# Softmax's division by the row sums: from a VectorE multiplication to a diagonal matrix in the transposing products

## The reference, cut to what matters

```python
def attend(q, k, v):
    s = jnp.einsum("bqkgd,bskd->bkgqs", q, k, preferred_element_type=F32) * (B_HEAD_DIM ** -0.5)
    p = jax.nn.softmax(s, axis=-1).astype(v.dtype)
    return jnp.einsum("bkgqs,bskd->bqkgd", p, v)
```

## Time and profile before

| | us |
|---|---|
| median of 3 runs | 2290.29 |
| lowest and highest of them | 2287.31, 2292.7 |
| the profiled execution, its own time | 2290.72 |
| its span, first to last instruction | 2288.9 |
| granted TensorE clock in it | 0.996 |

### The profile page before, as it was taken

The page is one execution under the profiler, slowest core; times in us unless marked ns, Lnnn a source line. Parts: engine busy times, 40 slices in busy tenths (PEclk is TensorE's granted clock), DMA queues, the critical chain, the costliest instruction groups (busy, mean ns, idle before and its releaser), DMA issues.

```text
span 2288.9 us, 41418 instructions
## 1 busy us (share of the span) xinstructions
PE 2220.6 (97%) x17332; PEld 2045.3 (89%) x17332; DVE 1618.4 (71%) x2749; ACT 1156.7 (51%) x1937; POOL 153.3 (7%) x142
## 2 busy tenths in 40 slices
PE   7999999999989999999999999999999999999998
PEld 3665889998879999999999989997779999999998
DVE  4399668655977645798557687577988557799654
ACT  3425445443365446756346564345556345957343
POOL 0013000000000000000000000015630000000000
PEclk9999999999999999999999999999999999999999
DMA  8148054555244554415554325562025554514552
GB/s 346 73 183 317 37 221 166 185 186 201 92 166 168 187 186 171 173 57 184 184 182 157 141 93 203 184 221 74 19 94 183 184 184 169 183 55 166 185 184 92
DMA packets 50873, 368.46 MB, mean 161 GB/s; under 512 B 5632, under 2 KB 5888, under 8 KB 6528
## 3 DMA queue, kind: packets, MB, share of 16 engines
q1 hardware_dynamic: 50544, 363.72, 43.2%
q10 hardware_dynamic: 144, 2.10, 0.2%
HBM read 364.75 MB, written 1.05 MB: 160 GB/s over the span
## 4 chain that ended last, share of the span: by engine, by line
PE 81%; DVE 11%; ACT 5%; issue 2%; DMA 0%; SPq 0%; DVEq 0%; POOL 0%; ACTq 0%
PE psum L263 67%; DVE weight_rest L257 2%; PE psum L4508 1%; PE psum L3069 1%; PE psum L4509 1%; ACT weight_parts L221 1%; PE psum L4530 1%; PE psum L3703 1%; PE psum L2719 1%; DVE work L2021 1%; PE psum L4544 1%; DVE work L3533 1%; DVE spare L2509 0%; DVE work L2508 0%; DMA weight_ring<-stream_dram 0%
## 5 line engine op out<-in xcount | busy, mean ns | idle before, releaser
L263 PE MATMUL psum<-input_parts,weight_parts 128*128 128x256 f32 x5184 | 933.0, 283 | 6.0 <-DVE work L1489 1.8
L263 PEld LDWEIGHTS psum<-input_parts,weight_parts 128*128 128x128 f32 x5184 | 801.0, 189 | 11.2 <-issue 5.3
L263 PE MATMUL psum<-input_parts,weight_rest 128*128 128x256 f32 x2592 | 733.6, 283 | 0.0
L257 DVE TENSOR_TENSOR weight_rest<-weight_ring,weight_parts 128x1024 fp32r<-128x1024 f32 x528 | 621.1, 1222 | 151.8 <-ACT weight_parts L221 151.3
L221 ACT ACTIVATE weight_parts<-weight_ring 128x1024 fp32r<-128x1024 f32 x540 | 538.1, 1051 | 128.2 <-PE psum L263 105.6
L263 PEld LDWEIGHTS psum<-input_parts,weight_rest 128*128 128x128 f32 x2592 | 488.9, 189 | 0.0
L263 PE MATMUL psum<-hidden_parts,weight_parts 128*128 128x256 f32 x2496 | 450.7, 283 | 2.6 <-DVE weight_rest L257 1.3
L263 PEld LDWEIGHTS psum<-hidden_parts,weight_parts 128*128 128x128 f32 x2496 | 385.1, 189 | 6.0 <-issue 3.4
L263 PE MATMUL psum<-hidden_parts,weight_rest 128*128 128x256 f32 x1248 | 352.2, 282 | 0.0
L263 PEld LDWEIGHTS psum<-hidden_parts,weight_rest 128*128 128x128 f32 x1248 | 235.0, 188 | 0.0
L1473 ACT ACTIVATE work<-psum 128x256 f32<-128x256 f32 x118 | 45.3, 384 | 352.3 <-PE psum L263 349.9
(11 more groups left out here) (532 smaller groups left out, 2855.4 us busy)
## 6 DMA issues: line engine op xcount, KB each, us to landing
weight_ring<-stream_dram SPq DMA_DIRECT2D x340, 1024.0 KB, 4.8
constants<-constants_dram SPq DMA_DIRECT2D x1, 2304.0 KB, 12.5
work<-s_bc_dram ACTq DMA_DIRECT2D x1, 2048.0 KB, 9.8
work<-ctx_dram SPq DMA_DIRECT2D x1, 1024.0 KB, 5.5
residual<-x_dram SPq DMA_DIRECT2D x1, 1024.0 KB, 7.6
work<-first_dram SPq DMA_DIRECT2D x1, 1024.0 KB, 14.9
out_dram<-residual SPq DMA_DIRECT2D x4, 256.0 KB, 2.1
vectors<-vectors_dram SPq DMA_DIRECT2D x1, 486.5 KB, 11.8
```

The lines of the kernel that those rows point to most:

```text
L257: ins = dve.tensor_tensor(self.rest[:, i % RING, cols], self.ring[:, i % RING, cols], self.parts[:, s % SPLITS, cols].bitcast(F32), ALU.su ...
L263: mm = pe.matmul(*args, **kw)
```

## The change

ScalarE writes the exponents to `probs` in SBUF, undivided. VectorE multiplies the 128x128 identity by the reciprocals instead, which gives a diagonal matrix for each unit in a new area `scales`, and the four transposes of a unit become four ordinary float32 products of the exponents with that matrix: they transpose and divide at once. The bank of the scores is now freed by ScalarE (`exp_done`), and ScalarE waits, from the fifth unit on, for the transposing products of the unit four earlier, since it now writes `probs`.

```diff
+        self.scales = k.area(AT_RS, 4, P)
...
-                self.score_jobs += [k.job(self.probs_ready[u]) for u in (2 * r, 2 * r + 1)]
+                self.score_jobs += [k.job(self.exp_done[u]) for u in (2 * r, 2 * r + 1)]
...
                     for s in range(4):
-                        mm = pe.transpose(self.turn_jobs[w].ap[:, s * P:(s + 1) * P],
-                                          self.probs[:, w % 4, s * P:(s + 1) * P], k.c("ident"))
+                        mm = pe.matmul(self.turn_jobs[w].ap[:, s * P:(s + 1) * P],
+                                       self.probs[:, w % 4, s * P:(s + 1) * P], self.scales[:, w % 4, :],
+                                       start=True, stop=True)
...
                     act.wait_ge(*self.peak[u])
-                    act.activation(self.score_jobs[u].ap[:, :], self.score_jobs[u].ap[:, :], ACT.Exp,
+                    if u >= 4:
+                        act.wait_ge(*self.turn_jobs[u - 4].full)
+                    act.activation(self.probs[:, u % 4, :], self.score_jobs[u].ap[:, :], ACT.Exp,
                                    bias=k.cols[:, 1, u:u + 1], scale=0.125, accum_out=k.cols[:, 2, u:u + 1])\
                        .then_inc(self.exp_done[u][0], 1)
...
-                    dve.tensor_scalar(self.probs[:, u % 4, :], self.score_jobs[u].ap[:, :], k.cols[:, 3, u:u + 1],
-                                      None, ALU.mult).then_inc(self.probs_ready[u][0], 1)
+                    dve.tensor_scalar(self.scales[:, u % 4, :], k.c("ident"), k.cols[:, 3, u:u + 1], None, ALU.mult)\
+                       .then_inc(self.probs_ready[u][0], 1)
```

## The result

| | runs | median, us | lowest and highest, us |
|---|---|---|---|
| before | 13 | 2288.29 | 2287.31, 2292.70 |
| after | 13 | 2293.81 | 2291.76, 2299.08 |

The account below looks back on a forecast made before the run. VectorE was taken to bound the attention until 212 us, TensorE from there to 233. A first-half -0.1 and a second-half +3.84 gave +3.7, on 2290.3 us 2294.0; range 2288.5 to 2298.0.

Parts of the forecast that it names:

- The transposing pairs: Two units' transposes on TensorE in rounds 1 to 8: 1.02 us becomes 1.98, +0.96 per pair, 3.84 in the second half.
- TensorE's way through the first half: Step-by-step TensorE starts up to the scores of round 5: longer pairs fill its waits at 195.57, 201.58 and 207.96.
- The 4.0 us saved on VectorE and the 3.84 us added on TensorE cancel ... Gain 0.1: First half of the attention: longer products fill TensorE's waits, VectorE then waits for TensorE; scores 5 at 212.1, not 212.19.
- The GpSimd rival: GpSimd's SBUF copies, 209.62 to 226.0, hold VectorE's new multiplication, decided in round 5: +5.1, 2295.4 us; chance 0.20.
- Hidden second pass: Products cost TensorE what transposes do, so VectorE's saving in the first half counts: -3.0, 2287.3 us; chance 0.10.
- nothing moves: A first-half saving of 2 to 4 us is given back in the second: 2290 to 2291 us; chance 0.08.
- The free multiplication: VectorE's new 128x128 multiplication from SBUF: 250 ns taken, bounds 153 and 348, saving 0.5 us each.
- The exponents: ScalarE's exponents, now PSUM to SBUF: 598 ns against 662, 0.06 us less each or at most as much more; costed at nothing.
- the added wait: ScalarE's exponents of unit u wait for the transposing products of u-4: costs nothing, as TensorE issues those a round before.
- both engines run at the full clock: VectorE and TensorE in the windows 186 to 212 and 212 to 233 us: 1.00 of 2.4 GHz.
- A pair four times as long: Skill's 4 times figure for FP32 transposes: a pair grows by some 2.8 us, giving about 2301; chance 0.02.
- The delay stays: Behind the attention TensorE leads the chain, so the +3.7 us is expected to last to the end.

## Why the prediction was right in its direction and short in its size

By the totals alone the forecast change of +3.7 lies inside the measured 3.4 to 7.3; it is the halves, +5.80, that show it short. That the forecast time came within 0.2 us of the measured one is luck: a median of before that was 2.0 us too high, and a change some 2 us too small.

- **The transposing pairs: right.** Forecast 1.98 us, measured 1.98 (215.51 in the chain). Forecast +3.84 for the second half, measured +3.78, and the same with the products alone. The rows of the delta rule were the right price; the first product stands 51.42 us after the scores of round 1 where 45.62 + 3.7 = 49.3 was forecast, and all of the miss is older than 211.50.
- **TensorE's way through the first half: right.** The scores of round 4 were forecast 1.26 late, 19.14 us behind those of round 1. They came 204.02 - 184.90 = 19.12 behind them. The waits at 195.57 and 201.58 went as said. That at 207.96, which was to go as well, left 0.63 us (205.78), since VectorE's line 478 stands behind the second held multiplication; with GpSimd one step later it is gone.
- **"The 4.0 us saved on VectorE and the 3.84 us added on TensorE cancel ... Gain 0.1": this is the step that failed.** Measured was a loss of 2.0. Without GpSimd the step holds: 24.28 and 24.29, a gain of 0.3. What is missing from it is GpSimd in round 3. VectorE's line 2034 releases GpSimd's clearing, and VectorE's next instructions are the two multiplications with their reciprocals. The multiplications took 1.92 and 1.80 us in place of 0.29 each, and line 482 then 1.92 in place of 0.17: 4.9 us in all, of which 2.3 reach the scores of round 5. How these 2.3 divide between the multiplications and line 482 no run shows: every run that freed the one freed the other. An estimate from the rows of after: the second multiplication ends at 205.61, so a free line 482 would have ended near 205.84 and the maxima begun near 205.9, where they began at 207.62. That makes some 0.6 for the multiplications and 1.7 for line 482, which meets the copy only because the multiplications push it behind the clearing. A multiplication on VectorE that reads the identity from a bank was not tried.
- **The GpSimd rival: the right mechanism at the wrong place.** The prediction looked at the copies, "209.62 to 226.0", and took round 5 to decide. It passed over the clearing just before them, and its sum asked of GpSimd only whether the copies end "early enough". It also says "I see no larger one-input instruction beside a copy". There was one, VectorE's transpose of line 2499 at 209.65 (2.19 us; 1.98 with GpSimd out of the way); it is hardly held and would have spoken against the rival. In before, the multiplication read from a bank and ran beside the clearing untouched, so nothing pointed there, save that clearing and multiplication start together there too (205.89 and 205.86, last section). At the places it named the holding did come (1.80 at 211.95, 1.44 at 216.37), but it cost nothing, as the runs with GpSimd later and one step later show. It costs 2.2 us where the pairs stay short, as the run with transposes kept shows. That the rival's +5.1 agrees with the measured total is chance: the loss came in another round.
- **Hidden second pass, nothing moves: both fell.** The pairs nearly doubled, and the first half gave nothing.
- **Sizes off, without effect.** The free multiplication takes 286 to 290 ns, not 250. The exponents take 687 ns, where 600 was the guess; that is inside the prediction's bound, 60 ns above 662. ScalarE still waits 14.5 us for maxima, and the added wait showed nowhere. The granted clock of the earlier trace rows is TensorE's alone, so the prediction's "both engines run at the full clock" is shown for TensorE only. A pair four times as long would add three times 1.02, 3.1 us, not 2.8; nothing hung on it.
- **The delay stays: right up to the next disturbance of the clock.** The attention of after starts 2.71 us earlier in its trace and its first product of the delta rule comes 3.09 later, which makes the 5.8; the measured +5.3 (3.4 to 7.3) agrees. The 3.09 later are still 3.16 at an instruction of VectorE at 1302.44 (1305.60 in after), and 1.64 at one at 1310.84 (1312.48): between 1300 and 1304 before was granted 0.50 and 0.65, and after the full clock.

## What to carry to other kernels

A stage with two engines near their limits takes little from a trade between them: here 0.46 us off each of two VectorE multiplications cost 0.96 us more on a TensorE pair, and in one half of the stage there was nothing to set against the cost. When an operation's source moves from a PSUM bank to SBUF, list what GpSimd does in SBUF from the first instruction after its release on, clearings as well as copies, and look at which VectorE instructions stand right behind the one that releases it. Moving the operation to an engine with idle time (ScalarE, 15 us of waits) gave the only version here whose stage became shorter without leaving work out.

## What the runs showed of the hardware that was not expected

- **The one-input multiplication on VectorE waits for GpSimd, for a clearing too.** A 128x128 multiplication from SBUF to SBUF, 0.29 us when free, took 1.92 and 1.80 beside two clearings, ending with each of them, and 1.2 to 2.1 beside most copies. Two of after took 0.29 there, at 211.55 and 215.58; the next copy starts at 211.63 and 215.73, so they fell where one copy gives way to the next. In before, the multiplications from a bank and line 482 ran beside the same clearing untouched (timeline of before, both engines):

```profile
205.86 0.75 DVE L2183 TENSOR_SCALAR work<-psum,columns 128x512 f32<-128x512 f32 x1
205.89 3.67 POOL L2456 MEMSET work<- 128x2048 f32 x2 [51.43 <-DVE work L2034]
...
207.85 0.17 DVE L482 TENSOR_TENSOR modulation<-modulation_turned,vectors 128x16 f32<-128x16 f32 x1
```

- Reading and writing SBUF is not enough to be held. The transpose of 128x1024 within SBUF (line 2499, in after 2503) took 1.93 us at 209.21 of after beside the copies and 1.98 with GpSimd out of the way, and the 128x1 multiplications within SBUF (line 2206) took 0.15 beside copies, as elsewhere.
- Line 482 has two inputs in SBUF: 0.17 us beside the clearing (207.85 above), which reads nothing, and 1.92 beside a copy. The Trainium skill, "SBUF — State Buffer", section on two separate sides, tells these apart: two SBUF inputs contend only with a GpSimd operation that reads SBUF, a two-port mode with any. The traces agree in both, if the one-input multiplication ran in such a mode, which no row shows directly.
- That section of the Trainium skill says that whichever starts first keeps the ports. Here the multiplication's record starts at 201.83 and the clearing's at 201.86, and still the multiplication ended after the clearing. The second run of after shows the same (205.53 and 205.57, 1.92 us). A start 0.03 us ahead in the records is thus no safety.
- Stretches at the lower clock (granted 0.61 and 0.54 above) come while TensorE is busy throughout (2.00 of 2 us). Before has them near 81, 1300, 1672 and 2044 us of its span, after near 680, 1674 and 2046: some places are common to both, others not. What one costs differs from place to place. That at 81 cost 1.7 us and that at 1300 cost 1.5 (the delay of after fell from 3.16 to 1.64). That at 680 cost some 0.1: VectorE's instructions come 3.07 us later than in before ahead of it (676.37 and 673.30) and 3.19 behind it (692.59 and 689.40), and TensorE's next products wait 0.20 for VectorE there. A stretch can thus cost a third of what the whole change costs, so two profiles are compared stage by stage.
